# Eight tiles of a weight ring set 4128 bytes apart instead of 4096

## The chip, the cores and the metric

The kernel runs on one core of one Trainium2 chip. Times are device microseconds (us) of one execution; the kernel before was timed twice. All engines work on the core's on-chip memory of 128 partitions (SBUF); "bytes apart" and "offset" below always mean bytes within one partition.

## The reference

One layer of a causal decoder trunk on 256 tokens of width 4096, all in float32. Nearly all of its work is products of the activations with large weights:

```
xn = rmsnorm(h, norm_mix)
(a_q, a_k, ... d_v) = split(xn @ w_in)            # 4096 x 5200
o_a, o_b, o_c, o_d = stick-breaking, top-k sparse, compressed/selected/window, dilated attention
z = xn @ gate_down                                # 4096 x 256
merged = sum_i sigmoid(z @ gate_up[i]) * (o_i @ w_branch_i)
h = h + merged @ w_out                            # 4096 x 4096
xn = rmsnorm(h, norm_ffn)
q = xn @ wq                                       # 4096 x 1024, then product-key top-16 of 4096 experts, 8 heads
act = gelu(xn @ u.T)                              # 4096 x 4096
h = h + scatter(gates * act at the picked experts) @ v   # 4096 x 4096
```

## The kernel before

The weights come from HBM as one stream of chunks. A chunk is 256 rows of a weight (two contraction tiles of 128, called j = 0 and 1) by 512 columns, 128 partitions x 1024 float32; in the very first group the columns are 336, so a chunk there is 128 x 672. The stream passes through a ring of RING = 4 slots with three tensors each, of 4096 bytes per partition and slot:

- `w_raw`: what the DMA of SyncE's queue writes (`load`, `load_in`). A slot's next DMA waits for `lo_ready` of the chunk that lay there.
- `w_hi`: ScalarE (ACT) copies `w_raw` to float32r, a float32 rounded for TensorE's single-pass product (line 1207; line 1566 for half a chunk). For chunk c it waits for the DMA and for `chunk_used >= c - 3`: TensorE must be through with chunk c - 4, which lay in the slot.
- `w_lo`: VectorE (DVE) writes `w_raw - w_hi`, the rounded-off rest (line 1616; line 2291 for half a chunk), after `hi_ready`.

The activations are split in the same way (`xt_hi`, `xt_lo`, `x_hi`, ...). TensorE (PE) forms each product from three: x_hi w_hi + x_lo w_hi + x_hi w_lo. The stationary operand is a 128x128 tile of the activations, loaded anew for every matmul (PEld in the rows); the moving operand is one half j of a ring slot, 512 columns. `products` issues 12 matmuls a chunk: four at line 676 (j = 0 and 1, each for the two token tiles h), four at line 679, four at line 683. `first_products` (lines 695, 699, 703) does the same for the group of 336 columns, `branch_products` (724, 726, 730) for the branches. In some stretches of the w_out and v products pairs of chunks are combined by a scheme with fewer products, which reads ring slots at lines 1079, 1080, 1085, 1160 and 1166 and sums `t_hi`, `t_lo` of ring data at lines 1038 to 1040; lines 1128 to 1130 close the last chunk with 256 columns at a time. In `out<-a,b` of the rows, a is the moving operand and b the stationary one.

The order on each engine is written out by hand, slot by slot; attention, the expert selection and the evacuations are placed between chunks. The memory is laid out by hand as well:

```python
    XT0 = base
    RG0 = XT0 + 64 * KB
    MG0 = RG0 + 12 * RING * KB
    CN0 = MG0 + 32 * KB
```

so `w_raw`, `w_hi` and `w_lo` are 16 KB each from RG0 on, and slot i begins 4096 i bytes into its tensor. Half j of a slot begins 2048 j bytes into it, in the group of 336 columns 1344 j bytes. The stationary tiles of `xt_hi` and `xt_lo` begin at multiples of 512 bytes from XT0. `t_hi` and `t_lo` stand at PJ0, which is 2048 bytes past CN0, at multiples of 2048 bytes from it. `cmp_bp`, a small bfloat16 operand of line 819, is read in runs of 45 columns that begin 90 bytes apart. `gate` begins at an offset of 128 bytes past a multiple of 512.

Of the kernel before, what the change touches and what calls it, by code (L numbers as in the profile page):

```python
# [20 lines left out]
F32 = mybir.dt.float32  # L21
F32R = mybir.dt.float32r
BF16 = mybir.dt.bfloat16
U32 = mybir.dt.uint32
ALU = mybir.AluOpType
ACT = mybir.ActivationFunctionType
AX = mybir.AxisListType.X

P = 128
# [39 lines left out]

RING = 4  # L70
LEAD = RING - 1
CPG = KT // 2
GRP = D // 512
MERGE = ("b", "c", "d", "a")
# [72 lines left out]
KB = 1024  # L147
# [46 lines left out]
PICKS_TURN = SOFTMAX_AT + 1  # L194
SCATTER_AT = PICKS_TURN + LEAD + 2
ROUND_AT = {SCATTER_AT + n * 3 // 2: n for n in range(ROUNDS)}
PUT_END = max(ROUND_AT) + LEAD + 1
WEIGH_AT = {max(PUT_END + 2 + q, CH_V + CPG // 2 + 3 + q - 14 if q >= 14 else 0): q for q in range(CPG)}
# [35 lines left out]
def build(nc, io):  # L234
# [1 line left out]
    base = (nc.sbuf_base + 31) // 32 * 32  # L236
    XT0 = base
    RG0 = XT0 + 64 * KB
    MG0 = RG0 + 12 * RING * KB
    CN0 = MG0 + 32 * KB  # L240

    def at(name, shape, dt, off):
        return nc.alloc_sbuf_tensor_at(name, shape, dt, offset=off)
# [3 lines left out]
    def const(name, shape, dt=F32):  # L247
        t = at(name, shape, dt, cursor[0])
        cursor[0] += (int(np.prod(shape[1:])) * 4 + 31) // 32 * 32
        assert cursor[0] <= nc.sbuf_usable_end, name  # L250
        return t
# [3 lines left out]
    xt_lo = at("xt_lo", [P, KT, S], F32R, XT0 + 32 * KB)  # L255

    w_raw = at("w_raw", [P, RING, 1024], F32, RG0)
    w_hi = at("w_hi", [P, RING, 1024], F32R, RG0 + 4 * RING * KB)
    w_lo = at("w_lo", [P, RING, 1024], F32R, RG0 + 8 * RING * KB)

    xt_raw = at("xt_raw", [P, KT, S], F32, MG0)
    rows = at("rows", [P, NT, D], F32, MG0)
# [10 lines left out]
    ident = const("ident", [P, P])  # L273
    g_mix = const("g_mix", [P, KT])
    g_ffn = const("g_ffn", [P, KT])
    small = const("small", [P, 320])
    PJ0 = cursor[0]

    proj = const("proj", [P, NT, NCOL])
# [143 lines left out]
    hi_ready, lo_ready, chunk_used = sems("hi_ready", "lo_ready", "chunk_used")  # L423
# [120 lines left out]

    MIX_OUT = {mix_end(b, n) + LEAD: (b, n) for b in MERGE for n in range(GRP)}
    GATE_OUT = {MIX_CH[b] + n * (1 + MIX_K[b] // 2) + LEAD: (b, n) for b in MERGE for n in range(GRP)}
    OUT_OUT = {CH_OUT + (n + 1) * CPG + LEAD: n for n in range(4, GRP)}

# [19 lines left out]
    with nc.Block() as block:  # L568
# [98 lines left out]
        def _(pe):  # L667
            def products(parity, chunk, slot, lhs, k0, width, first, last):

                wh = [w_hi[:, slot, j * width:(j + 1) * width] for j in range(2)]  # L670
                wl = [w_lo[:, slot, j * width:(j + 1) * width] for j in range(2)]
                o = [acc[:, parity, h, 0:width] for h in range(NT)]
                pe.wait_ge(hi_ready, chunk + 1)
                for j in range(2):
                    for h in range(NT):
                        pe.matmul(o[h], lhs(k0 + j, h)[0], wh[j], start=first and j == 0, stop=False)  # L676
                for j in range(2):
                    for h in range(NT):
                        pe.matmul(o[h], lhs(k0 + j, h)[1], wh[j], start=False, stop=False)  # L679
                pe.wait_ge(lo_ready, chunk + 1)  # L680
                for j in range(2):
                    for h in range(NT):
                        mm = pe.matmul(o[h], lhs(k0 + j, h)[0], wl[j], start=False, stop=last and j == 1)  # L683
                mm.then_inc(chunk_used, 1)

            def first_products(chunk, slot, width):

                pe.wait_ge(hi_ready, chunk + 1)
                wh = [w_hi[:, slot, j * width:(j + 1) * width] for j in range(2)]
                wl = [w_lo[:, slot, j * width:(j + 1) * width] for j in range(2)]  # L690
                k0, o = 2 * chunk, [acc[:, 0, h, 0:width] for h in range(NT)]
                for j in range(2):
                    pe.wait_ge(xt_hi_done, k0 + j + 1)
                    for h in range(NT):
                        pe.matmul(o[h], xt(k0 + j, h)[0], wh[j], start=k0 + j == 0, stop=False)
                for j in range(2):
                    pe.wait_ge(xt_lo_done, k0 + j + 1)
                    for h in range(NT):
                        pe.matmul(o[h], xt(k0 + j, h)[1], wh[j], start=False, stop=False)
                pe.wait_ge(lo_ready, chunk + 1)  # L700
                for j in range(2):
                    for h in range(NT):
                        mm = pe.matmul(o[h], xt(k0 + j, h)[0], wl[j], start=False, stop=k0 + j == KT - 1)
                mm.then_inc(chunk_used, 1)
# [7 lines left out]
            def branch_products(chunk, slot, lhs, k0, first, last, before):  # L712

                pe.wait_ge(hi_ready, chunk + 1)
                wh = [w_hi[:, slot, j * 512:(j + 1) * 512] for j in range(2)]
                wl = [w_lo[:, slot, j * 512:(j + 1) * 512] for j in range(2)]
                for h in range(NT):
                    if first and h == 0 and before:
                        pe.wait_ge(term_half, before)
                    elif first:  # L720
                        bank(0, (GN_MIX + 1) // 2 + before)
                    o = acc[:, 0, h, :]
                    for j in range(2):
                        pe.matmul(o, lhs(k0 + j, h)[0], wh[j], start=first and j == 0, stop=False)  # L724
                    for j in range(2):
                        pe.matmul(o, lhs(k0 + j, h)[1], wh[j], start=False, stop=False)  # L726
                    if h == 0:
                        pe.wait_ge(lo_ready, chunk + 1)
                    for j in range(2):
                        mm = pe.matmul(o, lhs(k0 + j, h)[0], wl[j], start=False, stop=last and j == 1)  # L730
                    if last and h == 0:
                        mm.then_inc(branch_half, 1)
                mm.then_inc(chunk_used, 1)
# [286 lines left out]
            for s in range(CH_MIX, CH_OUT):  # L1020
                b, n, j = mix_place(s)
# [18 lines left out]
                return pe.matmul(o, pair[0], moving[1][j], start=False, stop=stop)  # L1040

            def ring(slot):
                return [[w[:, slot, j * 512:(j + 1) * 512] for j in range(2)] for w in (w_hi, w_lo)]

            def wait_block(pair, i, h):

# [73 lines left out]
            def last_products(slot, kp):  # L1120

                for side_n in range(2):
                    cols = slice(side_n * 256, side_n * 256 + 256)
                    o = side[:, side_n, 0:256]
                    for j in range(2):
                        wh, wl = (w[:, slot, j * 512:(j + 1) * 512][:, cols] for w in (w_hi, w_lo))
                        xh, xl = xt(2 * kp + j, 1)
                        pe.matmul(o, xh, wh, start=j == 0, stop=False)
                        pe.matmul(o, xl, wh, start=False, stop=False)
                        mm = pe.matmul(o, xh, wl, start=False, stop=j == 1)  # L1130
                    if side_n == 0:
                        mm.then_inc(left_done, 1)
                return mm
# [63 lines left out]
        def _(act):  # L1197
# [4 lines left out]
            def hi(chunk, slot, width, m4):  # L1202

                act.wait_ge(raw_loaded[slot], raw_parts(m4) * 16)
                if not (isinstance(chunk, int) and chunk < RING):
                    act.wait_ge(chunk_used, chunk - (RING - 1))
                nc.scalar.activation(w_hi[:, slot, 0:width], w_raw[:, slot, 0:width], ACT.Copy).then_inc(hi_ready, 1)  # L1207


            def squares(i, ms):  # L1210
# [351 lines left out]
            def hi_half(chunk, slot):  # L1562

                act.wait_ge(raw_loaded[slot], raw_parts(chunk // RING) * 16)
                act.wait_ge(chunk_used, chunk - (RING - 1))
                nc.scalar.activation(w_hi[:, slot, 512:1024], w_raw[:, slot, 512:1024], ACT.Copy).then_inc(hi_ready, 1)

            def s_hi_part(i):

# [14 lines left out]
            for s in range(CH_F):  # L1584
# [6 lines left out]
                kp, i = placed(pair, s) if pair else (None, None)  # L1591
# [19 lines left out]
        def _(dve):  # L1611
            then = chain(dve, dve_chain)

            def lo(chunk, slot, width):
                dve.wait_ge(hi_ready, chunk + 1)
                nc.vector.tensor_tensor(w_lo[:, slot, 0:width], w_raw[:, slot, 0:width],  # L1616
                                        w_hi[:, slot, 0:width].bitcast(F32), ALU.subtract).then_inc(lo_ready, 1)

            def los(base_chunk, c0, c1, width=1024):
                for c in range(c0, c1):  # L1620
# [667 lines left out]
            def lo_half(chunk, slot):  # L2288

                dve.wait_ge(hi_ready, chunk + 1)  # L2290
                nc.vector.tensor_tensor(w_lo[:, slot, 512:1024], w_raw[:, slot, 512:1024],
                                        w_hi[:, slot, 512:1024].bitcast(F32), ALU.subtract).then_inc(lo_ready, 1)

            def block_rows_of(pair, i, h):

# [71 lines left out]
            for s in range(CH_V + 2 * CPG):  # L2367
# [7 lines left out]
                kp, i = placed(pair, s) if pair else (None, None)  # L2375
# [39 lines left out]
            for side_n in range(2):  # L2415
# [4 lines left out]
                cols = slice(side_n * 256, side_n * 256 + 256)  # L2420
# [154 lines left out]
```

## Time and profile before

| | |
|---|---|
| timed, median of 2 runs | 1907.34 us (1907.03 to 1907.64) |
| profiled execution, its own time | 1906.17 us |
| its span, first to last instruction | 1904.1 us |
| PE busy | 1899.7 us (100%), 8941 matmuls |
| PE loading weights (beside the matmuls) | 1566.8 us (82%) |
| DVE busy | 1463.1 us (77%) |
| ACT busy | 986.2 us (52%) |
| DMA | 412.69 MB, mean 217 GB/s |
| granted TensorE clock | 1.000 |

Busy time is the union of an engine's instructions. Matmuls overlap in a pipeline: the duration of one (389 ns for 512 columns) is its passage, and the distance of two starts is what it costs. A granted clock of 1.00 is 2.4 GHz, at which 512 columns take 213.3 ns, one column a cycle.

### The profile page before, as it was taken

What the parts mean: (1) busy time and instruction counts of PE and PEld (TensorE: products, weight loads), DVE (VectorE), ACT (ScalarE), POOL (GpSimd) and SP (SyncE); (2) the same over time, 40 slices, a digit from 0 to 9 for tenths busy, and PEclk for the clock granted to TensorE, in tenths of its full rate; (3) what the DMA queues carried; (4) which work ended last, traced back from release to release, by engine and by line L of the source; (5) the groups of instructions that cost most, each with busy time, mean ns of one, the idle gap of its engine ahead of it and who ended that gap; (6) DMA issues with size and microseconds to landing.
All of it is one profiled execution on the core that took longest, in us unless ns stands there. A gap on an engine that the chain in (4) does not pass through costs nothing.

```text
span 1904.1 us, 25847 instructions
## 1 busy us (share of the span) xinstructions
PE 1899.7 (100%) x8941; PEld 1566.8 (82%) x8941; DVE 1463.1 (77%) x2139; ACT 986.2 (52%) x1214; POOL 36.3 (2%) x49
## 2 busy tenths in 40 slices
PE   9999999999999999999999999999999999999999
PEld 8888888888888888888888888888887788888887
DVE  6578775585556889989765555899988878999897
ACT  6654644444456655556454464444444455555553
POOL 0010010000000000000000000000000000000000
PEclk9999999999999999999999999999999999999999
DMA  9976667655655668877787776767766678666664
GB/s 321 353 223 166 167 177 202 172 157 157 190 178 175 186 189 289 271 235 233 258 252 239 216 226 218 233 209 214 222 204 194 198 205 290 222 215 222 217 221 155
DMA packets 198833, 412.69 MB, mean 217 GB/s; under 512 B 45793, under 2 KB 124257, under 8 KB 198081
## 3 DMA queue, kind: packets, MB, share of 16 engines
q1 hardware_dynamic: 174048, 369.35, 63.3%
q10 hardware_dynamic: 20976, 25.19, 3.9%
q0 software_dynamic: 3696, 16.65, 2.5%
q8 instruction: 71, 1.16, 0.2%
q14 instruction: 42, 0.34, 0.1%
HBM read 390.15 MB, written 20.97 MB: 216 GB/s over the span
## 4 chain that ended last, share of the span: by engine, by line
PE 99%; DMA 0%; SPq 0%; ACT 0%; DVE 0%; issue 0%
PE acc L676 25%; PE acc L679 25%; PE acc L683 25%; PE acc L724 3%; PE acc L726 3%; PE acc L730 3%; PE acc L1160 2%; PE side L1038 1%; PE side L1040 1%; PE side L1039 1%; PE acc L1166 1%; PE acc L1080 1%; PE acc L1085 1%; PE acc L1079 1%; PE side L854 1%; PE side L966 1%
## 5 line engine op out<-in xcount | busy, mean ns | idle before, releaser
L1616 DVE TENSOR_TENSOR w_lo<-w_raw,w_hi 128x1024 fp32r<-128x1024 f32 (+1 forms) x649 | 784.8, 1213 | 386.7 <-ACT w_hi L1207 381.9
L1207 ACT ACTIVATE w_hi<-w_raw 128x1024 fp32r<-128x1024 f32 (+1 forms) x649 | 681.0, 1052 | 690.6 <-PE acc L683 572.2
L676 PE MATMUL acc<-w_hi,xt_hi 128*128 128x512 f32 x1348 | 365.6, 393 | 0.0
L679 PE MATMUL acc<-w_hi,xt_lo 128*128 128x512 f32 x1348 | 360.7, 389 | 0.0
L683 PE MATMUL acc<-w_lo,xt_hi 128*128 128x512 f32 x1348 | 360.5, 389 | 0.0
L679 PEld LDWEIGHTS acc<-w_hi,xt_lo 128*128 128x128 f32 x1348 | 253.0, 188 | 53.3
L683 PEld LDWEIGHTS acc<-w_lo,xt_hi 128*128 128x128 f32 x1348 | 253.1, 188 | 53.0
L676 PEld LDWEIGHTS acc<-w_hi,xt_hi 128*128 128x128 f32 x1348 | 250.1, 188 | 51.5 <-issue 1.8
L676 PE MATMUL acc<-w_hi,x_hi 128*128 128x512 f32 x640 | 175.1, 395 | 0.0
L679 PE MATMUL acc<-w_hi,x_lo 128*128 128x512 f32 x640 | 171.5, 390 | 0.0
L683 PE MATMUL acc<-w_lo,x_hi 128*128 128x512 f32 x640 | 171.4, 390 | 0.0
L679 PEld LDWEIGHTS acc<-w_hi,x_lo 128*128 128x128 f32 x640 | 120.1, 188 | 25.7
L683 PEld LDWEIGHTS acc<-w_lo,x_hi 128*128 128x128 f32 x640 | 120.1, 188 | 25.6
L676 PEld LDWEIGHTS acc<-w_hi,x_hi 128*128 128x128 f32 x640 | 117.2, 188 | 22.2
L1560 ACT ACTIVATE t_hi<-t_raw 128x1024 fp32r<-128x1024 f32 x46 | 47.7, 1058 | 24.6 <-PE acc L1040 14.9
L2285 DVE TENSOR_TENSOR t_lo<-t_raw,t_hi 128x1024 fp32r<-128x1024 f32 x46 | 54.1, 1218 | 0.0
L1349 ACT ACTIVATE gate<-acc 128x512 f32<-128x512 f32 x64 | 34.8, 596 | 37.3 <-PE acc L683 37.3
L676 PE MATMUL acc<-w_hi,zt_hi 128*128 128x512 f32 x128 | 34.5, 391 | 0.0
L683 PE MATMUL acc<-w_lo,zt_hi 128*128 128x512 f32 x128 | 34.2, 389 | 0.0
L679 PE MATMUL acc<-w_hi,zt_lo 128*128 128x512 f32 x128 | 34.2, 389 | 0.0
L2271 DVE TENSOR_TENSOR t_raw<-w_raw 128x1024 f32<-128x1024 f32 x23 | 28.1, 1221 | 3.9 <-DMA w_raw<-in_stream 3.5
L1861 DVE TENSOR_TENSOR gate<-acc,gate 128x512 f32<-128x512 f32 x48 | 30.7, 681 | 0.0
(376 smaller groups left out, 2050.2 us busy)
## 6 DMA issues: line engine op xcount, KB each, us to landing
w_raw<-in_stream SPq DMA_DIRECT2D x504, 512.0 KB, 4.2
w_raw<-in_w_in SPq DMA_DIRECT2D x16, 496.0 KB, 4.0
w_raw<-in_w_in SPq DMA_DIRECT2D x16, 480.0 KB, 4.1
w_raw<-in_w_in SPq DMA_DIRECT2D x16, 464.0 KB, 3.8
w_raw<-in_w_in SPq DMA_DIRECT2D x16, 448.0 KB, 3.9
w_raw<-in_w_in SPq DMA_DIRECT2D x16, 432.0 KB, 3.8
w_raw<-in_w_in SPq DMA_DIRECT2D x16, 416.0 KB, 4.1
w_raw<-in_w_in SPq DMA_DIRECT2D x16, 400.0 KB, 3.8
```

Of the source, the lines that this page charges most:

```text
L676: pe.matmul(o[h], lhs(k0 + j, h)[0], wh[j], start=first and j == 0, stop=False)
L679: pe.matmul(o[h], lhs(k0 + j, h)[1], wh[j], start=False, stop=False)
L683: mm = pe.matmul(o[h], lhs(k0 + j, h)[0], wl[j], start=False, stop=last and j == 1)
L724: pe.matmul(o, lhs(k0 + j, h)[0], wh[j], start=first and j == 0, stop=False)
L726: pe.matmul(o, lhs(k0 + j, h)[1], wh[j], start=False, stop=False)
L730: mm = pe.matmul(o, lhs(k0 + j, h)[0], wl[j], start=False, stop=last and j == 1)
L1160: pe.matmul(o, xt(2 * kp + j, h)[p], w[0][j], start=kp == 1 and h == 1 and p == 0 and j == 0, stop=False)
L1207: nc.scalar.activation(w_hi[:, slot, 0:width], w_raw[:, slot, 0:width], ACT.Copy).then_inc(hi_ready, 1)
L1349: e = nc.scalar.activation(gate[:, n % 2, h, :], acc[:, 1, h, :], ACT.Sigmoid)
L1560: nc.scalar.activation(flat(hi_tile[:, d]), flat(raw[:, d]), ACT.Copy).then_inc(t_hi_done, 1)
L1616: nc.vector.tensor_tensor(w_lo[:, slot, 0:width], w_raw[:, slot, 0:width], w_hi[:, slot, 0:width].bitcast(F32), ALU.subtract).then_inc(lo_ ...
L2285: nc.vector.tensor_tensor(flat(lo_tile[:, d]), flat(raw[:, d]), flat(hi_tile[:, d]).bitcast(F32), ALU.subtract).then_inc(t_lo_done, 1)
```

## The change

`w_hi` and `w_lo` become lists of four tiles each. Tile n of the eight (hi 0 to 3, lo 0 to 3) is moved up by 32 n bytes, so that neighbours begin 4128 bytes apart: hi by 0, 32, 64 and 96 bytes, lo by 128, 160, 192 and 224. `w_raw` keeps its place. All that is laid out from MG0 on (`xt_raw`, `rows`, the features, `probs`, `wmat`, `s_hi`, `ident`, the two gain vectors, `small`) moves up by 256 bytes; `small` loses 64 unused columns (256 bytes), so PJ0 and all that follows stays where it is. No instruction, wait, size or order changes. The diff, with the hunks left out that only write `w_hi[slot][:, ...]` for `w_hi[:, slot, ...]` (and the same for `w_lo`) in `first_products`, `branch_products`, the paired products and the half chunks:

```diff
@@ -69,6 +69,7 @@
 
 RING = 4
 LEAD = RING - 1
+RING_SKEW = (0, 32, 64, 96, 128, 160, 192, 224)
 CPG = KT // 2
 GRP = D // 512
 MERGE = ("b", "c", "d", "a")
@@ -236,7 +237,7 @@
     base = (nc.sbuf_base + 31) // 32 * 32
     XT0 = base
     RG0 = XT0 + 64 * KB
-    MG0 = RG0 + 12 * RING * KB
+    MG0 = RG0 + 12 * RING * KB + 256
     CN0 = MG0 + 32 * KB
 
     def at(name, shape, dt, off):
@@ -255,8 +256,8 @@
     xt_lo = at("xt_lo", [P, KT, S], F32R, XT0 + 32 * KB)
 
     w_raw = at("w_raw", [P, RING, 1024], F32, RG0)
-    w_hi = at("w_hi", [P, RING, 1024], F32R, RG0 + 4 * RING * KB)
-    w_lo = at("w_lo", [P, RING, 1024], F32R, RG0 + 8 * RING * KB)
+    w_hi, w_lo = ([at(f"{name}{i}", [P, 1024], F32R, RG0 + 4 * (first + i) * KB + RING_SKEW[first - RING + i])
+                   for i in range(RING)] for name, first in (("w_hi", RING), ("w_lo", 2 * RING)))
 
     xt_raw = at("xt_raw", [P, KT, S], F32, MG0)
     rows = at("rows", [P, NT, D], F32, MG0)
@@ -273,7 +274,7 @@
     ident = const("ident", [P, P])
     g_mix = const("g_mix", [P, KT])
     g_ffn = const("g_ffn", [P, KT])
-    small = const("small", [P, 320])
+    small = const("small", [P, 256])
     PJ0 = cursor[0]
 
     proj = const("proj", [P, NT, NCOL])
@@ -667,8 +668,8 @@
         def _(pe):
             def products(parity, chunk, slot, lhs, k0, width, first, last):
 
-                wh = [w_hi[:, slot, j * width:(j + 1) * width] for j in range(2)]
-                wl = [w_lo[:, slot, j * width:(j + 1) * width] for j in range(2)]
+                wh = [w_hi[slot][:, j * width:(j + 1) * width] for j in range(2)]
+                wl = [w_lo[slot][:, j * width:(j + 1) * width] for j in range(2)]
                 o = [acc[:, parity, h, 0:width] for h in range(NT)]
                 pe.wait_ge(hi_ready, chunk + 1)
                 for j in range(2):
@@ -1123,7 +1124,7 @@
                     cols = slice(side_n * 256, side_n * 256 + 256)
                     o = side[:, side_n, 0:256]
                     for j in range(2):
-                        wh, wl = (w[:, slot, j * 512:(j + 1) * 512][:, cols] for w in (w_hi, w_lo))
+                        wh, wl = (w[slot][:, j * 512:(j + 1) * 512][:, cols] for w in (w_hi, w_lo))
                         xh, xl = xt(2 * kp + j, 1)
                         pe.matmul(o, xh, wh, start=j == 0, stop=False)
                         pe.matmul(o, xl, wh, start=False, stop=False)
...
```

## Rows read from the trace of the kernel before

**Rows 1.** The page: span, busy time, granted clock, the chain that ended last.

```profile
span 1904.1 us, 25847 instructions
...
PE 1899.7 (100%) x8941; PEld 1566.8 (82%) x8941; DVE 1463.1 (77%) x2139; ACT 986.2 (52%) x1214; POOL 36.3 (2%) x49
...
PE 99%; DMA 0%; SPq 0%; ACT 0%; DVE 0%; issue 0%
```

**Rows 2.** Waits of PE: who was waited for, us in total, times, longest.

```profile
PE side L710 <- DVE warm L2363: 1.3, 1, 1.3
PE acc L695 <- ACT w_hi L1207: 0.5, 1, 0.5
```

**Rows 3.** Timeline of PE in the v products: start, us, instruction, count.

```profile
1635.36 0.39 PE L1038 MATMUL side<-t_hi,s_hi 128*128 128x512 f32 x1
...
1638.08 1.07 PE L676 MATMUL acc<-w_hi,xt_hi 128*128 128x512 f32 x4
...
1639.89 1.07 PE L683 MATMUL acc<-w_lo,xt_hi 128*128 128x512 f32 x4
...
1648.96 0.61 PE L1160 MATMUL acc<-w_hi,xt_hi 128*128 128x512 f32 x2
```

**Rows 4.** PE in the group of 336 columns; 72 starts from first to last.

```profile
19.89 0.78 PE L695 MATMUL acc<-w_hi,xt_hi 128*128 128x336 f32 x4
...
30.93 0.78 PE L695 MATMUL acc<-w_hi,xt_hi 128*128 128x336 f32 x4
```

**Rows 5.** PE at the end, 256 columns; nine starts from first to last.

```profile
1900.11 0.28 PE L1130 MATMUL side<-w_lo,xt_hi 128*128 128x256 f32 x1
...
1901.19 0.28 PE L1130 MATMUL side<-w_lo,xt_hi 128*128 128x256 f32 x1
```

**Rows 6.** PE in two narrow windows: bfloat16 products of 96 and 45 columns.

```profile
1401.47 0.51 PE L966 MATMUL side<-hot_q,hot_c 128*128 128x96 bf16 x8
1401.80 0.70 PE L676 MATMUL acc<-w_hi,x_hi 128*128 128x512 f32 x2
...
188.28 1.08 PE L819 MATMUL side<-cmp_bp,cmp_pc 128*128 128x45 bf16 x36
```

**Rows 7.** Groups of PE's instructions: count, busy us, mean ns, idle before.

```profile
L676 PE MATMUL acc<-w_hi,xt_hi 128*128 128x512 f32 x1348 | 365.6, 393 | 0.0
...
L683 PE MATMUL acc<-w_lo,xt_hi 128*128 128x512 f32 x1348 | 360.5, 389 | 0.0
L676 PE MATMUL acc<-w_hi,x_hi 128*128 128x512 f32 x640 | 175.1, 395 | 0.0
```

**Rows 8.** PE's readers of w_lo, first and last of 14 rows (2567 matmuls).

```profile
L683 PE MATMUL acc<-w_lo,xt_hi x1348: 388/389/398, 38.3 to 1892.8; 128*128 128x512 f32 x193
...
L1130 PE MATMUL side<-w_lo,xt_hi x4: 279/283/283, 1900.1 to 1901.2; 128*128 128x256 f32 x4
```

**Rows 9.** Timeline in the projection: ACT, then DVE, make a chunk.

```profile
60.24 1.06 ACT L1207 ACTIVATE w_hi<-w_raw 128x1024 fp32r<-128x1024 f32 x1 [2.89 <-DMA w_raw<-in_w_in]
...
61.34 1.23 DVE L1616 TENSOR_TENSOR w_lo<-w_raw,w_hi 128x1024 fp32r<-128x1024 f32 x1 [2.73 <-ACT w_hi L1207]
```

**Rows 10.** By stretch of 100 us: PE, PEld, DVE, ACT, POOL, clock, DMA.

```profile
900.00:1000.00 100.00, 100.00 (x443) 82.81 (x442) 69.74 (x86) 49.28 (x58) 2.84 (x4) 1.00 0.80 253
1300.00:1400.00 100.00, 100.00 (x446) 82.85 (x445) 91.75 (x237) 44.43 (x44) 0.00 (x0) 1.00 0.73 222
1700.00:1800.00 100.00, 100.00 (x443) 82.84 (x442) 90.33 (x96) 54.59 (x57) 1.43 (x2) 1.00 0.67 215
```

**Rows 11.** DVE's line 1616 alone in one of those stretches.

```profile
1300.00:1400.00 100.00, 45.27 (x37) 1.00 0.73 222
```

**Rows 12.** Single lines: duration of one in ns, minimum, median, maximum.

```profile
L1616 DVE TENSOR_TENSOR w_lo<-w_raw,w_hi x607: 1176/1225/1230, 100.4 to 1891.8; 128x1024 fp32r<-128x1024 f32 x152
...
L2285 DVE TENSOR_TENSOR t_lo<-t_raw,t_hi x46: 1214/1218/1221, 1623.1 to 1877.9; 128x1024 fp32r<-128x1024 f32 x46
...
L1875 DVE TENSOR_TENSOR rows<-rows,gate x16: 1224/1225/1228, 598.3 to 705.6; 128x1024 f32<-128x1024 f32 x16
```

More of the change, by code:

```diff
@@ L688, in first_products @@
                 pe.wait_ge(hi_ready, chunk + 1)
-                wh = [w_hi[:, slot, j * width:(j + 1) * width] for j in range(2)]
-                wl = [w_lo[:, slot, j * width:(j + 1) * width] for j in range(2)]
+                wh = [w_hi[slot][:, j * width:(j + 1) * width] for j in range(2)]
+                wl = [w_lo[slot][:, j * width:(j + 1) * width] for j in range(2)]
                 k0, o = 2 * chunk, [acc[:, 0, h, 0:width] for h in range(NT)]
@@ L714, in branch_products @@
                 pe.wait_ge(hi_ready, chunk + 1)
-                wh = [w_hi[:, slot, j * 512:(j + 1) * 512] for j in range(2)]
-                wl = [w_lo[:, slot, j * 512:(j + 1) * 512] for j in range(2)]
+                wh = [w_hi[slot][:, j * 512:(j + 1) * 512] for j in range(2)]
+                wl = [w_lo[slot][:, j * 512:(j + 1) * 512] for j in range(2)]
                 for h in range(NT):
@@ L1042, in ring @@
             def ring(slot):
-                return [[w[:, slot, j * 512:(j + 1) * 512] for j in range(2)] for w in (w_hi, w_lo)]
+                return [[w[slot][:, j * 512:(j + 1) * 512] for j in range(2)] for w in (w_hi, w_lo)]
             def wait_block(pair, i, h):
@@ L1206, in hi @@
                     act.wait_ge(chunk_used, chunk - (RING - 1))
-                nc.scalar.activation(w_hi[:, slot, 0:width], w_raw[:, slot, 0:width], ACT.Copy).then_inc(hi_ready, 1)
+                nc.scalar.activation(w_hi[slot][:, 0:width], w_raw[:, slot, 0:width], ACT.Copy).then_inc(hi_ready, 1)
             def squares(i, ms):
@@ L1565, in hi_half @@
                 act.wait_ge(chunk_used, chunk - (RING - 1))
-                nc.scalar.activation(w_hi[:, slot, 512:1024], w_raw[:, slot, 512:1024], ACT.Copy).then_inc(hi_ready, 1)
+                nc.scalar.activation(w_hi[slot][:, 512:1024], w_raw[:, slot, 512:1024], ACT.Copy).then_inc(hi_ready, 1)
             def s_hi_part(i):
@@ L1615, in lo @@
                 dve.wait_ge(hi_ready, chunk + 1)
-                nc.vector.tensor_tensor(w_lo[:, slot, 0:width], w_raw[:, slot, 0:width],
-                                        w_hi[:, slot, 0:width].bitcast(F32), ALU.subtract).then_inc(lo_ready, 1)
+                nc.vector.tensor_tensor(w_lo[slot][:, 0:width], w_raw[:, slot, 0:width],
+                                        w_hi[slot][:, 0:width].bitcast(F32), ALU.subtract).then_inc(lo_ready, 1)
             def los(base_chunk, c0, c1, width=1024):
@@ L2290, in lo_half @@
                 dve.wait_ge(hi_ready, chunk + 1)
-                nc.vector.tensor_tensor(w_lo[:, slot, 512:1024], w_raw[:, slot, 512:1024],
-                                        w_hi[:, slot, 512:1024].bitcast(F32), ALU.subtract).then_inc(lo_ready, 1)
+                nc.vector.tensor_tensor(w_lo[slot][:, 512:1024], w_raw[:, slot, 512:1024],
+                                        w_hi[slot][:, 512:1024].bitcast(F32), ALU.subtract).then_inc(lo_ready, 1)
             def block_rows_of(pair, i, h):
```

## Prediction

> **What bounds the kernel now.** I read the page first: PE has 1899.7 of the span's 1904.1 us and 99% of the chain that ended last, at a granted clock of 1.00 throughout [rows 1, 10]. The waits come second: PE waited 1.3 us for the warm-up's data and 0.5 us for `w_hi` at the start, and for nobody after that [rows 2]. So no buffer, transfer or other engine sets the end. What sets it is the distance at which TensorE starts one matmul after another, and only a change of that distance, or a wait that is new, can move the time.
>
> A busy share of 100% does not say that this distance is the shortest possible, so the third view is the timeline. In the v products, 48 matmuls of 512 columns start between 1638.08 and 1648.96 us: 10.88 / 48 = 226.7 ns each [rows 3]. At 2.4 GHz 512 columns are 213.3 ns, so each carries 13.3 ns beyond its columns. The change can gain only if some of these 13.3 ns come from where the operands lie.
>
> How much hangs on that: `w_lo` is read by 2567 matmuls [rows 8], `w_hi` by twice as many (two of each three products), together 7701 of 8941. The whole excess is 7701 x 13.3 = 103 us, 5.4% of the span. That is why the question deserves work although nothing waits.
>
> **What the change touches on TensorE.** Three comparisons within this trace say whether the 13.3 ns depend on the address.
>
> First, another width. In the group of 336 columns, 72 matmuls start within 30.93 - 19.89 = 11.04 us, 153.3 ns each [rows 4]; 336 columns are 140.0 ns, and the excess is again 13.3 ns. At the end of the kernel, with 256 columns, nine take 1.08 us, 120.0 ns each against 106.7 ns of columns: 13.3 ns once more [rows 5]. A reader held up by collisions in memory would be held up in proportion to what it reads; 2048 bytes and 1024 bytes a partition carry the same excess. It is a fixed cost of one float32r matmul with its own weight load.
>
> Second, another address. In the group of 336 columns half 1 starts 1344 bytes into its slot, which is 64 bytes past a multiple of 128, whereas half 0 starts at the slot's beginning. Half of the 72 matmuls thus already run with a moving operand set off against the stationary one, as the change will set it off, and the mean is that of the stretches in which everything starts at multiples of 512 bytes. The timeline resolves 0.01 us in 72, 0.14 ns; were the offset half different, it would be by less than 0.3 ns.
>
> Third, another place. The 12 matmuls that move `t_hi` and `t_lo` (nine against `s_hi` and `s_lo`, three against `xt`) lie between the starts at 1635.36 and 1638.08 us, 226.7 ns each [rows 3]. They read no tile of the ring. And that pace is the same in a stretch where DVE is busy for 70% of the time and the DMA engines for 80% as in one with 90% and 67%: 443 matmuls in 100 us in both [rows 10]. Neighbours' traffic does not show in it.
>
> The Trainium skill, "TensorE: Matmul & The Clock Gate", section "Back-to-back issue gap", gives N / 2.4 + 2.5 ns, which would be 215.8 ns here; this trace's bfloat16 products of 96 columns agree with that form (below), its float32r products do not. By the page 10.9 ns a matmul, 84 us in all, would be there to be had, if the rest were address collisions; this is a rival below.
>
> I therefore take zero for the change of pace on PE. Bounds: below, the first four matmuls of a chunk average 393 ns at line 676 where line 683 shows 389, and 395 in the w_q and u products [rows 7], that is 4 x 1348 + 6 x 640 = 9.2 us of stretched passages. If all of that were collisions with writers, the change could give back 9 us; it sits on the first of three lines that read the same tiles, line 679 reads `w_hi` too and shows 389, so it belongs to the start of a chunk and not to the tile. Above: half of the eight tiles now begin at an odd multiple of 32 bytes, and with the slots used in turn some 3850 matmuls read from such a start. No float32r row has one. The nearest is line 819, whose runs of 45 bfloat16 columns begin 90 bytes apart, at all kinds of addresses: 36 in 1.08 us from the first start to the last end, and with a passage of 0.18 us at the end 0.90 / 35 = 25.7 ns each, 6.9 ns beyond 18.8 ns of columns [rows 6]. The 96-column products, all at multiples of 64 bytes, take (1401.80 - 1401.47) / 8 = 41.2 ns, 1.2 ns beyond their 40. If the difference of 5.7 ns were due to the start and not to so narrow a matmul, it would cost 5.7 x 3850 = 22 us. I take zero here as well, since the offset half of the 336-column group is a product of the same kind; the ends are -9 and +22 us.
>
> **What the change touches on ACT and DVE.** The copy to `w_hi` writes, and the subtraction to `w_lo` reads and writes, at an address whose offset against `w_raw` differs from slot to slot. Line 1616 has a median of 1225 ns with everything at multiples of 2048 bytes from each other. Line 1875, with the same count of elements and one of its inputs 128 bytes off such a multiple, has 1225 ns too, and line 2285 has 1218 [rows 12]. So I expect 0 +- 10 ns an instruction. Nothing of it reaches the end. After TensorE leaves chunk c - 4, ACT may start on chunk c, while TensorE still has three chunks of 12 x 226.7 ns = 2.72 us, 8.16 us in all, before it needs the result; ACT and DVE are through 62.57 - 60.24 = 2.33 us after ACT starts [rows 9]. As a question of throughput the tightest stretch is 1300 to 1400 us, where DVE has 8.25 us left, and line 1616 45.27 us of work [rows 10, 11]: it would have to become 18% slower (223 ns each) to bound there. Cost at the cover that there is: nothing. With no cover, 10 ns on 680 chunks would be 7 us.
>
> **What the change touches elsewhere.** No instruction, wait or queue changes; `w_raw`, the target of the DMAs, stays. The 256 bytes by which `xt_raw`, `rows`, `wmat` and the others move keep them at multiples of 256, so they are costed at nothing, with the reasons of the third comparison. The start, where PE waited 1.8 us in all [rows 2], may shift by a few tenths.
>
> The Trainium skill, "SBUF — State Buffer", section "Who interferes with whom", says that "PE and ACT never wait on anyone", and the trace's even pace agrees. The same page counts cachelines of 16 bytes, of which 32 is a multiple; by it no operand is split otherwise than before.
>
> **The sum.** Own time of the profiled execution 1906.2 us + 0 (PE) + 0 (ACT, DVE, covered) + 0 (start) = 1906.2; the median of the runs is 1.2 us above it, so the forecast is 1907.3 us.
>
> **The rivals.** *Nothing to measure* is my forecast: the 13.3 ns are TensorE's own. 0.93.
>
> *The excess is a collision after all.* The stationary tile and the moving half now begin at the same offset modulo 512 bytes, and the load of the next weights runs beside the matmul for 82% of the time [rows 1]. If each matmul lost its 13.3 ns at the start because both reads meet in one part of the memory, that too would be independent of width. The seven shifted tiles of eight would be freed: 7/8 x 103 = 90 us, 1817 us. Against it stands the offset half in the 336-column group, which shows the full excess. 0.03. By the skill's "TensorE: Matmul & The Clock Gate" and its section quoted above a remainder of 2.5 ns would stay, and the case would come to 7/8 x 84 = 73 us, 1834 us.
>
> *Odd starts cost.* This one ends on the other side. A moving run that begins at an odd multiple of 32 bytes might need one more access, and TensorE takes it at every matmul on the four tiles skewed by 32, 96, 160 and 224. If it costs as much as the fixed excess, 13.3 x 3850 = 51 us, 1958 us. It decides from 38 us, that is from 9.9 ns a matmul; line 819 bounds the likely price at 5.7 ns. 0.04.
>
> **How the numbers follow.** The range holds the first case with its bounds: 9 us down is possible only if all stretched passages are collisions, so I go down to 1900; 22 us up is the end of a price that I doubt, so I go up by half of it, rounded, to 1918. The two others have 0.07 together and stay outside. 2% of 1907 us is 38 us, about what a measurement of this kernel can tell from no change: faster 0.03, same 0.93, slower 0.04.
>
> **What the profile of the changed kernel would show.** Right: 48 matmuls of a like stretch in 10.88 us, 443 matmuls in 100 us, line 1616 at 1225 ns and line 1207 unchanged, no new waits of PE. The second case would show 213 to 218 ns between starts and more waits for `lo_ready`; the third a pace that alternates by slot, 226.7 ns in the tiles of even skew and more in the others. I'd be wrong in the reasons, though not in the time, if line 1616 or 1207 changed by tens of ns by slot. The forecast is most exposed to what no row of float32r shows, the odd 32-byte start.

## The result, and the profile after

The changed kernel takes 1945.76 us (median of 2 runs, 1945.58 to 1945.95) against 1907.34: ratio 1.0204, 95% interval 1.0179 to 1.0228. It is slower by 38 us, and outside the range of 1900 to 1918. That it is slower is clear of the noise; whether by more than the 2% at which the chances were set is not, since the interval holds 1.02.

The page of the changed kernel, as [rows 1]:

```profile
span 1943.6 us, 25847 instructions
...
PE 1939.7 (100%) x8941; PEld 1569.1 (81%) x8941; DVE 1464.4 (75%) x2139; ACT 987.2 (51%) x1214; POOL 36.5 (2%) x49
...
PE 100%; DVE 0%; issue 0%
```

The same instructions in the same numbers; DVE and ACT worked 1.3 and 1.0 us longer in all, PE 40.0 us. The waits of PE, as [rows 2]:

```profile
PE side L711 <- DVE warm L2364: 1.3, 1, 1.3
```

No new wait took anything; the one of 0.5 us for `w_hi` at the start even went. So PE is slower while it waits for nobody. By stretch, as [rows 10] (PE, PEld, DVE, ACT, POOL, clock, DMA):

```profile
900.00:1000.00 100.00, 100.00 (x432) 80.91 (x431) 73.05 (x90) 48.80 (x56) 2.12 (x3) 1.00 0.76 240
1300.00:1400.00 100.00, 100.00 (x432) 80.84 (x431) 93.61 (x283) 40.05 (x40) 0.00 (x0) 1.00 0.71 214
1700.00:1800.00 100.00, 100.00 (x433) 81.09 (x432) 90.10 (x96) 54.08 (x57) 1.43 (x2) 1.00 0.65 215
```

432 and 433 matmuls in 100 us where there were 443 to 446, at the same granted clock of 1.00 (2.4 GHz): 231 instead of 226 ns a start, with all kinds of matmuls counted. The timeline shows how it is spread. Four chunks of the projection, one for each slot of the ring, beginning with slot 0 (start, us, instruction, count), as [rows 3]:

```profile
114.53 1.08 PE L677 MATMUL acc<-w_hi,xt_hi 128*128 128x512 f32 x4
115.45 1.07 PE L680 MATMUL acc<-w_hi,xt_lo 128*128 128x512 f32 x4
116.36 1.09 PE L684 MATMUL acc<-w_lo,xt_hi 128*128 128x512 f32 x4
117.28 1.09 PE L677 MATMUL acc<-w_hi,xt_hi 128*128 128x512 f32 x4
...
120.09 1.10 PE L677 MATMUL acc<-w_hi,xt_hi 128*128 128x512 f32 x4
...
122.88 1.10 PE L677 MATMUL acc<-w_hi,xt_hi 128*128 128x512 f32 x4
...
125.70 1.08 PE L677 MATMUL acc<-w_hi,xt_hi 128*128 128x512 f32 x4
```

The four chunks take 2.75, 2.81, 2.79 and 2.82 us; before, each took 2.72. In all 11.17 / 48 = 232.7 ns against 226.7, 6.0 ns a matmul. Slot 0, whose hi tile has a skew of 0, loses least: the four at line 680 take 0.91 us as before, the four before them on the same tile and the four on its lo tile (128 bytes) 0.92 each. Over the whole kernel, the distance between the starts of consecutive float32r matmuls of 512 columns rose from a mean of 228.6 to 233.6 ns (some hundred distances above 300 ns are in both means, 35 us in each kernel, which is why the first is above 226.7); with 7869 of them (7497 on the ring, 372 on `t_hi`, `t_lo` and the like of the w_out products) 5.0 x 7869 = 39 us, the whole loss.

### The profile page after: what moved, and what is told of

Read it like the earlier page. It is cut to its first block, busy times and chain, and to the rows that moved or that the text cites. A ratio compares the mean times of both kernels' runs of the same rounds, so it can differ in the third digit from the quotient of the medians.

```text
span 1943.6 us, 25847 instructions
## 1 busy us (share of the span) xinstructions
PE 1939.7 (100%) x8941; PEld 1569.1 (81%) x8941; DVE 1464.4 (75%) x2139; ACT 987.2 (51%) x1214; POOL 36.5 (2%) x49
## 4 chain that ended last, share of the span: by engine, by line
PE 100%; DVE 0%; issue 0%
PE acc L677 26%; PE acc L684 25%; PE acc L680 25%; PE acc L727 3%; PE acc L725 3%; PE acc L731 3%; PE acc L1161 2%; PE side L1040 1%; PE side L1041 1%; PE side L1039 1%; PE acc L1167 1%; PE acc L1086 1%; PE acc L1080 1%; PE acc L1081 1%; PE side L855 1%; PE side L967 1%
## 5 line engine op out<-in xcount | busy, mean ns | idle before, releaser
L677 PE MATMUL acc<-w_hi,xt_hi 128*128 128x512 f32 x1348 | 373.1, 398 | 0.0
L684 PE MATMUL acc<-w_lo,xt_hi 128*128 128x512 f32 x1348 | 368.7, 395 | 0.0
L680 PE MATMUL acc<-w_hi,xt_lo 128*128 128x512 f32 x1348 | 367.2, 394 | 0.0
L1292 ACT ACTIVATE probs<-probs,small 128x128 f32<-128x128 f32 (+2 forms) x44 | 18.3, 417 | 22.0 <-DVE small L1775 21.9
```

## The experiments

The theories: A, the distance of two starts depends on the offset between the moving run and the stationary tile, within TensorE alone; B, TensorE's reads collide with what ACT, DVE or the DMAs write; C, the moving run's own address counts; D, the spacing of 4128 bytes between the ring's tiles counts. All kernels but the three maps compute the whole layer; their edits are made in the changed kernel unless something else is said, and "matmuls in 100 us" are those from 900 to 1000 us, as in [rows 10]. A ratio compares with runs of the kernel before that were made beside the experiment: their medians were 1906.28 us for the first three, 1906.56 for lo256 and ring64, 1906.47 for lo64. The maps leave all of it out: TensorE works on tiles of random data, at addresses like the kernel's (stationary tiles from XT0, moving runs 64 KB above), with the weights loaded anew for each matmul.

**The layout without the skews (layout_only).**

```diff
-RING_SKEW = (0, 32, 64, 96, 128, 160, 192, 224)
+RING_SKEW = (0, 0, 0, 0, 0, 0, 0, 0)
```

> The changed kernel with all eight skews at 0 and the 256 bytes in front of MG0 kept. It separates the ring from what lies behind it. Theory A (the distance of two matmul starts grows with the offset between the moving run and the stationary tile, TensorE alone): ring pace back at 226.7 ns, only the products against s_hi and s_lo, which stay 256 bytes off, at 230 to 231 ns; some 400 of them x 4 ns = 1.6 us, so 1908 to 1910 us. Theory B (collisions of TensorE's reads with the writes of ACT, DVE and DMA): the ring's tiles are back on the same footing, 1907 to 1910 us as well. If the displaced rest were the cause of the loss: about 1945 us.

Measured 1907.08 us, ratio 1.0001 (0.9992 to 1.0011), 443 matmuls in 100 us:

```profile
900.00:1000.00 100.00, 100.00 (x443) 82.81 (x442) 70.82 (x87) 49.87 (x60) 2.12 (x3) 1.00 0.81 258
```

The whole loss is the skews' own. The expected 230 ns against `s_hi` did not come: with the ring at 0 those products have 226.7 ns, though `s_hi` stands 256 bytes off. In the changed kernel the products on `t_hi` and `t_lo`, which read no tile of the ring, had 229.9 ns: they were slowed by the skewed matmuls around them.

**All eight tiles by the same 128 bytes (ring128).**

```diff
+RING_SKEW = (128, 128, 128, 128, 128, 128, 128, 128)
```

> All eight tiles moved by the same 128 bytes, so they are 4096 bytes apart again but stand off the stationary tiles. Theory A: every ring matmul pays what the tile with a skew of 128 bytes paid, 231 against 226.7 ns, so 7500 x 4.3 = 32 us, 1936 to 1944 us. Theory D (what costs is the spacing of 4128 bytes between the ring's own tiles, that is which of them are read and written at once): 1907 to 1910 us. Theory C (the moving run's own address, whatever the stationary's): slower as by A.

Measured 1948.82 us, ratio 1.0223 (1.0206 to 1.0240), 431 matmuls in 100 us:

```profile
900.00:1000.00 100.00, 100.00 (x431) 80.61 (x430) 72.77 (x90) 48.90 (x58) 2.12 (x3) 1.00 0.74 234
```

The tiles are 4096 bytes apart and the kernel is as slow as the changed one. D falls. The loss of 42.5 us is 5.7 ns for each of the 7497 matmuls, above the 4.3 ns that I had expected by A: the price read off slot 0's lo tile was too low.

**Everything by 96 bytes (all96).** The kernel before with one edit:

```diff
-    base = (nc.sbuf_base + 31) // 32 * 32
+    base = (nc.sbuf_base + 31) // 32 * 32 + 96
```

> The kernel before with every tile in memory moved up by 96 bytes: all offsets between tiles as before, all absolute addresses off. Theory A (relation of moving to stationary): 1907 us, pace 226.7 ns. Theory C (absolute start address): the hi tile with a skew of 96 bytes had about 235 ns between starts, so 7500 x 8 = 60 us more, about 1967 us, and at least 1930 us.

Measured 1906.53 us, ratio 1.0000 (0.9990 to 1.0010), 443 matmuls in 100 us. C falls: what counts is the relation of addresses.

**The map of offsets (map).** Its core; `case` moves the moving operand by m bytes and the stationary by s, 48 matmuls each, `odd` and `even` alternate as output so that the blocks stand apart in the trace:

```python
case(0, 0, 512)
for c in [(m, 0, 512) for m in range(0, 1056, 32)] + [(0, s, 512) ...] + [(v, v, 512) ...] + ...: case(*c)
# then, with ACT and DVE copying tiles without a pause: (0, 0), (64, 0), (128, 0), (0, 0)
```

> No part of the layer: 52 blocks of 48 matmuls of float32r in the chunk's order of operands, on random data, with ACT and DVE idle, then four blocks with both copying 4096-byte tiles all the time; the output is not the reference's. Blocks 1 to 33 move the moving operand by 0, 32, 64, ... 1024 bytes at a fixed stationary tile; then the stationary is moved alone, then both alike, then 256 and 336 columns. Theory A: 226.7 ns at 0, 230 to 236 ns at most other offsets with ACT and DVE idle too, both moved alike back at 226.7, and a period in the offset, 512 bytes if the stationary's width sets it. Theory B: 226.7 ns in every quiet block, more only in the busy ones. Theory C: both moved alike is as slow as the moving one alone.

The timeline of PE; the first rows shown are m = 0, 32, 64, 96, 128 and 160, then from 110.29 us m = 256 and 288:

```profile
21.18 11.04 PE L83 MATMUL even<-m_all,s_all 128*128 128x512 f32 x48
32.06 11.37 PE L83 MATMUL odd<-m_all,s_all 128*128 128x512 f32 x48
43.26 11.16 PE L83 MATMUL even<-m_all,s_all 128*128 128x512 f32 x48
54.26 11.37 PE L83 MATMUL odd<-m_all,s_all 128*128 128x512 f32 x48
65.47 11.36 PE L83 MATMUL even<-m_all,s_all 128*128 128x512 f32 x48
76.67 11.40 PE L83 MATMUL odd<-m_all,s_all 128*128 128x512 f32 x48
...
110.29 11.05 PE L83 MATMUL even<-m_all,s_all 128*128 128x512 f32 x48
121.18 11.37 PE L83 MATMUL odd<-m_all,s_all 128*128 128x512 f32 x48
```

A block's pace is the distance to the next block's start over 48: 10.88 us (226.7 ns) at 0, 11.20 (233.3) at 32, 11.00 (229.2) at 64, 11.21 (233.5) at 96, 11.20 (233.3) at 128, and 10.89 us again at 256. Offsets from 256 to 1024 repeat this. Moving the stationary tile alone by 128 bytes (the row at 422.18 us) costs likewise, 11.15 us; by 256 (433.33 us) it costs nothing. Nor does moving both by 64, 96 or 128, as the rows from 466.31 us show (10.92, 10.91 and 10.92 us):

```profile
422.18 11.32 PE L83 MATMUL even<-m_all,s_all 128*128 128x512 f32 x48
433.33 11.05 PE L83 MATMUL odd<-m_all,s_all 128*128 128x512 f32 x48
...
466.31 11.08 PE L83 MATMUL even<-m_all,s_all 128*128 128x512 f32 x48
477.23 11.08 PE L83 MATMUL odd<-m_all,s_all 128*128 128x512 f32 x48
488.14 11.07 PE L83 MATMUL even<-m_all,s_all 128*128 128x512 f32 x48
499.06 11.05 PE L83 MATMUL odd<-m_all,s_all 128*128 128x512 f32 x48
```

And the blocks with both neighbours at work, m = 0, 64, 128, 0 (in the last one the copies end within its first 4 us):

```profile
553.20 11.09 PE L83 MATMUL odd<-m_all,s_all 128*128 128x512 f32 x48
564.12 11.17 PE L83 MATMUL even<-m_all,s_all 128*128 128x512 f32 x48
575.12 11.32 PE L83 MATMUL odd<-m_all,s_all 128*128 128x512 f32 x48
586.28 11.09 PE L83 MATMUL even<-m_all,s_all 128*128 128x512 f32 x48
```

10.92, 11.00 and 11.16 us. The second and third are no more than in quiet (11.00 and 11.20). The first is 0.04 us more than in quiet, but so are the quiet blocks with both operands moved alike, and for the same reason: after some changes of offset the first seven to nine distances are uneven, 224 to 236 ns, and then they are 226 to 227 again, here with the neighbours still at work. (After others, as from 224 to 256 bytes, only the first is.) So neither ACT nor DVE costs anything; no DMA ran here. A holds, B falls as far as it speaks of ACT and DVE, and the period is 256 bytes, not the 512 that I had offered.

Two of the uneven stretches say more. Between the blocks with both moved by 64 and by 96 bytes, and again between 96 and 128, the operands of every matmul start in line; only at the border is the first stationary tile of the new block loaded beside the last moving run of the old one, 32 bytes off. Yet the distance over the border is 235 ns, and those after it are 230, 224, 231, 236, 228, 233 and 231 ns, 34 ns too much in all. And 128 bytes have two paces, 233.3 ns in the row at 65.47 us and 232.4 in those at 422.18 and 575.12 us: one offset can settle at either. What decides between them no run shows.

**256 bytes in the kernel (lo256).**

```diff
+RING_SKEW = (0, 0, 0, 0, 256, 256, 256, 256)
```

> The changed kernel with skews 0, 0, 0, 0 for the hi tiles and 256 for the four lo tiles. The map of offsets had a period of 256 bytes. If the period carries over to the kernel (theory A256: only the offset modulo 256 bytes between moving run and stationary tile counts): 226.7 ns and 1906 to 1909 us, although the lo tiles lie as far off as the last skewed one did. If any offset other than a multiple of 512 or 1024 costs, as the single tile width of 512 bytes would suggest: 2500 lo matmuls x 4 to 6 ns = 10 to 15 us, 1917 to 1922 us.

Measured 1906.07 us, ratio 0.9998 (0.9988 to 1.0008), 442 matmuls in 100 us. The period holds in the kernel.

**64 bytes throughout (ring64).**

```diff
+RING_SKEW = (64, 64, 64, 64, 64, 64, 64, 64)
```

> All eight tiles moved by 64 bytes, the cheapest offset of the map (228.9 ns between starts against 226.7; 128 bytes had 233.4, or 232.0 in the kernel). Theory A256 with the map's price: 7500 x 2.2 = 17 us, so 1921 to 1926 us. If the cost grew with the distance from 0 or were the same for any offset, the kernel would lie between 1930 and 1950 us. If a writer's collisions set it (theory B), the map's price, made with ACT and DVE idle, would not hold.

Measured 1923.73 us, ratio 1.0089 (1.0069 to 1.0109), 438 matmuls in 100 us:

```profile
900.00:1000.00 100.00, 100.00 (x438) 82.00 (x437) 70.16 (x81) 48.95 (x57) 2.12 (x3) 1.00 0.78 246
```

The map's price for this offset carries over.

**The fine map (map_fine).**

> No part of the layer, no output of it: blocks of 32 matmuls as in the first map, ACT and DVE idle. Offsets of the moving operand in steps of 4 bytes up to 252, then 256 columns at eight offsets, then 320 to 496 columns, then bfloat16 with 512 columns at 0, 32, 64, 128 and 16 bytes. Theory A256: 226.7 ns is the least at 512 columns and multiples of 256 bytes are the only such points; every other offset gives 228 to 236 ns. If some offset gave less than 226.7 ns, a version faster than both kernels would exist. The two reads can only disturb each other if both run at float32's rate: for bfloat16 I expect 215 to 217 ns at every offset.

The 56 offsets between the multiples of 32 bytes gave 228.2 (at 108 bytes) to 240.0 ns (at 116, 132 and 196), as means of the starts after the first five in a block; I had expected 236 at most. None was below 226.7. The blocks of 256 columns are the surprise; rows of PE's timeline for offsets 0, 32, 64, 96 and then 192 and 224, 32 matmuls each:

```profile
445.89 4.00 PE L73 MATMUL odd<-m_all,s_all 128*128 128x256 f32 x32
449.72 3.94 PE L73 MATMUL even<-m_all,s_all 128*128 128x256 f32 x32
453.50 3.93 PE L73 MATMUL odd<-m_all,s_all 128*128 128x256 f32 x32
457.27 3.99 PE L73 MATMUL even<-m_all,s_all 128*128 128x256 f32 x32
...
468.65 3.81 PE L73 MATMUL odd<-m_all,s_all 128*128 128x256 f32 x32
472.30 3.94 PE L73 MATMUL even<-m_all,s_all 128*128 128x256 f32 x32
```

3.83 us (119.7 ns) at offset 0, but 3.65 us (114.1 ns; 113.3 once settled) at 192 bytes: at this width the common start is not the best. The widths between, at 0, 64 and 128 bytes, settle at:

| columns | 0 | 64 | 128 bytes | columns alone |
|---|---|---|---|---|
| 320 | 146.7 | 146.6 | 146.7 ns | 133.3 ns |
| 384 | 173.3 | 173.3 | 175.9 | 160.0 |
| 448 | 202.6 | 200.0 | 203.7 | 186.7 |

At 320 columns these offsets change nothing; at 448 the common start costs 16 ns beyond the columns and 64 bytes are better. (480 and 496 columns gave 216.7 to 217.6 and 223.2 to 224.5 ns; there half 1 is never in line with half 0.) The last blocks are bfloat16, 512 columns, at 0, 32 and 64 bytes, 6.91 us or 215.9 ns each:

```profile
568.60 7.08 PE L73 MATMUL even<-m_half,s_half 128*128 128x512 bf16 x32
575.51 7.07 PE L73 MATMUL odd<-m_half,s_half 128*128 128x512 bf16 x32
582.42 7.07 PE L73 MATMUL even<-m_half,s_half 128*128 128x512 bf16 x32
589.33 7.07 PE L73 MATMUL odd<-m_half,s_half 128*128 128x512 bf16 x32
```

**Mixed offsets and the kernel's own order (map_mix).**

```python
for slot in range(4):
    for part in range(3):                       # lines 677, 680, 684 of the changed kernel
        skew = order[slot + 4 * (part == 2)]    # four matmuls at a time
```

> No part of the layer, no output of it, ACT and DVE idle. First 513 blocks of 16 matmuls of 512 columns in which three offsets run through 0, 32, ... 224 bytes each: of the moving operand as a whole, of its half 1 against half 0, of the stationary tile h = 1 against h = 0. Then the kernel's own order of operands, twelve matmuls a chunk through four slots, 144 matmuls for each of six sets of skews, the change's among them. Theory A256 with a carry from one matmul to the next: the change's skews give here, without any neighbour, the medians of the changed kernel (slot 0: hi 227, lo about 231; slot 1: 233.6; slot 2: 233; slot 3: 234 to 235), a mean of 232 to 233 ns. If the map's single prices simply held by tile, slot 2's hi tiles (64 bytes) would be at 229. Of the mixed blocks I expect none below 226.7 ns; one at 222 ns or less would be a kernel 2% faster than both.

Of the 512 combinations the one without any offset had 226.6 ns, the other 511 lay between 228.3 and 235.4 (means of all 16 distances of a block). The third cycle of the change's skews, with no other engine at work, is in the first four rows here, twelve matmuls of one slot a row; the fifth begins the next set, in which all skews are 0:

```profile
1935.86 2.91 PE L57 MATMUL odd<-m_all,s_all 128*128 128x512 f32 x12
1938.60 2.97 PE L57 MATMUL even<-m_all,s_all 128*128 128x512 f32 x12
1941.41 2.96 PE L57 MATMUL odd<-m_all,s_all 128*128 128x512 f32 x12
1944.20 2.98 PE L57 MATMUL even<-m_all,s_all 128*128 128x512 f32 x12
1947.02 2.89 PE L57 MATMUL odd<-m_all,s_all 128*128 128x512 f32 x12
```

11.16 us for 48, 232.5 ns each, against the changed kernel's 11.17. Matmul by matmul the distances to the next start (ns, medians; in the kernel over the chunks from 40 to 500 us) agree too:

```
slot 0   changed kernel  233 231 227 227   227 227 227 227   234 224 237 229
         map_mix         233 230 226 227   226 226 227 226   234 224 237 229
slot 3   changed kernel  236 235 232 240   233 236 232 237   234 234 233 234
         map_mix         236 235 232 240   233 237 231 237   234 234 233 234
```

TensorE with its two operands, at these offsets and in this order, is the whole of the loss; no DMA ran here either, so the rest of B falls too. Slot 0's first two distances show the carry: they belong to matmuls at offset 0, and pay for what went before.

**Only the lo tiles by 64 bytes (lo64).**

```diff
+RING_SKEW = (0, 0, 0, 0, 64, 64, 64, 64)
```

> The changed kernel with skews 0 for the hi tiles and 64 for the lo tiles: a third of the ring's matmuls stands 64 bytes off, two thirds stand at 0. Single prices by tile: 2567 x 2.4 ns = 6 us, 1912 to 1914 us. If the matmuls at 0 that follow skewed ones are slowed too, as the unskewed products on t_hi were in the changed kernel, more: with all of them at 229 it is 1923 us as in the run with 64 throughout, and more than that if a switch of offset costs by itself.

Measured 1935.76 us, ratio 1.0155 (1.0138 to 1.0172), 435 matmuls in 100 us:

```profile
900.00:1000.00 100.00, 100.00 (x435) 81.32 (x434) 72.08 (x87) 49.05 (x57) 2.13 (x3) 1.00 0.76 242
```

29 us for a third of the matmuls, more than the 17 us of 64 bytes throughout, and above both prices that I had named for a case without a cost of the switch (1912 to 1914 and 1923 us). In map_mix the same order gave a mean of 231.1 ns, of which (231.1 - 226.7) x 7500 = 33 us. A switch of offset costs by itself, on both sides of it: in map_mix the eight matmuls at offset 0 of a chunk have distances of 231, 236, 228, 233, 230, 227, 227 and 226 ns, the four at 64 bytes after them 237, 235, 232 and 231, where a steady 64 bytes have 228.9.

## Why the prediction was wrong

**What failed is "the 13.3 ns are a fixed cost of one float32r matmul with its own weight load".** The excess changes with the offset at 512 columns from 13.3 ns at 0 to 26.7 ns at some offsets, at 256 columns from 13.3 down to 6.7 ns at 192 bytes, and by a few ns at 384 and 448. It isn't even the same at every width with a common start: 16 ns at 448 columns. I had three widths and took equal excesses for a constant. The products of 512 and 256 columns stood at starts that the layout had put in line, so they could not tell "no effect of the address" from "the address is right everywhere"; the third width was the exception, and the next paragraph is about it.

**The second comparison was the weak one.** The half that starts 1344 bytes into the slot is 64 bytes off modulo 256, so it did show an offset, but at 336 columns, where the first map has 152.6 ns with the halves as in the kernel before and 154.4 with both moved by a further 64 bytes. In the changed kernel, 48 matmuls of that group, one round of the four slots from 21.51 us on, took 7.42 us, 154.6 ns, instead of 153.3: 1.3 ns, about a quarter of what 512 columns lose. The width in the trace was a less sensitive one, and I carried its "less than 0.3 ns" over to another width. The group also held no block without an offset half to compare with, and no run has one, so what the offset half costs at 336 columns stays open.

**The third comparison** (the same pace beside busier neighbours) was right and stays right: in the map ACT and DVE at full work cost nothing at the offsets tried, and map_mix, with no neighbour and no DMA, has the kernel's pace. It spoke against theory B, not against an effect within TensorE.

**The bounds.** The upper one of 22 us came from a bfloat16 row; bfloat16 shows no effect in the fine map (512 columns, five offsets), so it bounded nothing. Halving it for the range had no row behind it either. It also charged half of the tiles, those at odd multiples of 32 bytes; even multiples pay as well (128 bytes: 42.5 us throughout). The term "zero for the change of pace on PE" measured +5.0 ns on 7869 matmuls. The lower bound, 9 us of stretched first passages, was not touched: the first line of a chunk shows 393 ns against 389 at the second in the kernels at offset 0, and 398 against 394 in the changed one, 4 ns more in both.

**The rivals.** The mirror of what happened stood there as "the excess is a collision after all", with both operands starting at the same offset named as its condition, and the sign assumed: that reads in line collide and reads out of line don't. At 512 columns it is the other way round, for each of the 567 sets of offsets that the two later maps tried. Its price counted tiles, not matmuls: the one unshifted tile is a hi tile, and those are read twice as often, so 5/6 of 103 us, 86 us, would have been freed, not 7/8. "Odd starts cost" had the sign and roughly the size (51 us against 38) with the wrong condition: what counts is the offset between the operands, not the start of one of them. That its number came near is luck; 64 and 128 bytes, even multiples of 32, cost 17 and 42.5 us when the whole ring has them.

**What held:** line 1617 at its old median, line 1208 too (1062 ns against 1061 at line 1207 before), no bound on DVE or ACT, no new wait, no cost at the start, none for the 256 bytes behind the ring:

```profile
L1617 DVE TENSOR_TENSOR w_lo<-w_raw,w_hi x649: 850/1225/1229, 6.2 to 1931.1; 128x1024 fp32r<-128x1024 f32 x159, 128x672 fp32r<-128x672 f32 x4
```

What stays open is what inside the chip repeats every 256 bytes. That the stationary tile's read meets the moving run's is inferred from three findings (only the difference of the two addresses counts, of the two types tried float32r alone is affected, a matmul pays for offsets before it, even where only a load and its neighbour's moving run were out of line); no run watches the reads themselves. The first map's trace adds that the weight load begins 3 ns after the matmul before it and takes 188 ns at every offset, while the matmul's own passage grows from 389 to 395 ns. In the bfloat16 blocks the load takes 98 ns, so whether the type, its bytes or the shorter load saves them is open too. The Trainium skill says, in "TensorE: Matmul & The Clock Gate", section "Step-by-step: what each phase is for", that loading the next tile's weights does not take read bandwidth from the running matmul. The bfloat16 blocks agree with that (215.9 ns at every offset). The float32r blocks don't, if the inference is right: with the stationary tile alone moved by 128 bytes the pace went from 226.7 to 232.4 ns, and the measurement decides.

## What to carry to other kernels

A unit that is busy 100% of the time and waits for nobody can still be slowed by layout: measure the distance of starts, not the waits. For float32r products of 512 columns with a fresh stationary tile each, keep moving runs and stationary tiles at the same start modulo 256 bytes, and check it after every edit of the memory map; having only some of them out of line isn't the cheaper way: a third of the matmuls at 64 bytes cost 29 us, all of them 17 us. At another width, measure first. And equal readings at several sizes are no proof of a constant when the suspected cause stood at the same value in all of them; the first map of offsets, in an otherwise empty kernel, took 0.6 ms of chip time and showed the effect and its period.

## What the runs showed of the hardware

- Float32r, 512 columns, weights loaded anew: 226.7 ns at a common start modulo 256 bytes, 228.2 to 240.0 ns at the 4-byte offsets between the multiples of 32, 228.9 (64 bytes) to 234.2 ns (160 bytes) at those multiples; bfloat16: 215.9 ns at all of five offsets.
- The same at 256 columns: 120.0 ns at a common start, 113.3 ns at 192 bytes; at 448 columns 202.6 and, at 64 bytes, 200.0; at 320 columns 146.7 at 0, 64 and 128 bytes. The best offset depends on the width.
- A change of offset from one matmul to the next can disturb up to nine that follow, those at offset 0 too: skewing a third of the ring's matmuls (29 us) cost more than skewing all by the same amount (17 us).
